# Six empty token columns taken out of a one-core streaming encoder: 1056 columns in chunks of 352 in place of 1062 in chunks of 354

## The chip, the cores and the metric

The kernel runs on one core of one Trainium2 chip. The metric is the device time of one execution in microseconds (us); the time of a kernel is the median over its runs, and one further execution was taken by the profiler. Engines are named as in the profile: PE is TensorE (PEld its weight loads), DVE VectorE, ACT ScalarE, POOL GpSimd, SP SyncE.

## The reference, cut to what matters

Two requests share one set of weights: a prompt of 1024 tokens and a sample of 32 tokens, each token a vector of 1024 features. Two layers:

- Layer 0: RMSNorm, an input projection into a state-space mixer and a windowed attention, an output projection, residual add.
- Layer 1: RMSNorm, then a short gated convolution: `z = C * V`, causal depthwise `conv3(z)` of width 3, times `B`, output projection, residual add.
- Both layers: RMSNorm, 4-head cross-attention into 256 memory tokens, residual add; RMSNorm, then a gated feed-forward of width 2816: `silu(conv3(h @ w_gate)) * (h @ w_val)`, down projection, residual add.
- A last RMSNorm.

The two convolutions run along tokens. The prompt's starts from two zero columns, the sample's from two stored columns, so that the two requests need two columns ahead of each.

## The kernel before, in words

Features lie on the 128 partitions, tokens along the free dimension: `X[P, 8, TW]` holds eight feature blocks of `TW` columns. `TW` is 1062: columns 0 to 1023 are the prompt, 1024 to 1029 (`SEQ:S0`) are empty, 1030 to 1061 the sample. Every product runs over all `TW` columns, cut into `NCH` = 3 chunks of `CW` = 354, one bank of PSUM each; six of the eight banks are two sets of three (`pset(0)`, `pset(1)`), which tiles use in turn.

Matrix products are in fp32 with both operands split in a high and a low part (`XH`, `XL` for activations, `WH`, `WL` for weights; `HH`, `HL` for the hidden values). So each step of a product is three matmuls, by `mms` (L981 to L983): high by high, low by high, high by low, each with a weight load of its own of 128x128.

- `tile_a` (used for up projections): 8 feature blocks x 3 chunks x 3 = 72 matmuls into one set.
- `down_tile` (down projections): 2 x 3 x 3 = 18 matmuls into one set.
- Weights stream from HBM in blocks: SP loads `WR`, ACT makes `WH` (L1672), POOL makes `WL` (L1575).

The phases follow in a fixed order: memory keys and values (`kv`), input projection and mixers (`inp`, `outb`, `glu`, `outa`), cross-attention `x0`, feed-forward `f0`, gated convolution `c1`, `x1`, `f1`. Each engine runs its own list, written out by hand; between engines there are semaphores. The class `Steps` gives the n-th increment of a semaphore a name, so `v.at("gate0", g)` is the point at which the step `gate0` of iteration `g` is done.

In a feed-forward group `g` (11 groups of two hidden blocks `e` = 0, 1) PE runs: gate tile of e = 0, the eight down tiles of the group before, value tile of e = 0, gate tile of e = 1, value tile of e = 1. DVE takes the gate tile out of PSUM into `G` (L864), makes the three taps of the convolution (`conv_taps`, L836 to L849: copy of the three tap weights to `FW`, copy of the two stored columns into `G`, one `tensor_scalar` and two `scalar_tensor_tensor` over `TW` columns into `TAP`), adds the down tiles to `X` (L891) in between, scales the SiLU that ACT made (L871), takes the value tile (L876) and makes the low part `HL` (L880). In the buffer `G` a block has `TW` + 2 columns: two zero columns, the prompt, and the stored columns of the sample in the last two of the six empty ones. PE waits for DVE where a set of banks must be free: the third down tile of a group, for one, waits for the add of the first (`(add[q], g * 8 + (j - 9))`).

The gated convolution `c1` has the same frame, with `C2` as the first product (L929), `G` as the second (L936), the taps, a scaling by `RSTD` in `TAP` (L939), and `HID` (L942).

Where the columns `SEQ:S0` would hold stale values, they are set to zero: `HH` and `HL` ahead of each cross-attention (L735, L736), `GY` in the first mixer (L716).

The names that the prediction follows: `CW`, `TW`, `S0` (L29 to L32), `mms`, `tile_a`, `down_tile` on PE, `gate`, `taps`, `scale`, `hid`, `tile` and `conv_taps` on DVE.

Of the kernel before, what the change touches and what calls it, by code (L numbers as in the profile page):

```python
# [21 lines left out]
ALU = mybir.AluOpType  # L22
# [3 lines left out]
P = 128  # L26
D, KT = 1024, 8
SEQ, DEC = 1024, 32
NCH, CW = 3, 354  # L29
TW = NCH * CW  # L30
# [63 lines left out]
def build(nc, a):  # L94
    with ExitStack() as ctx:
# [131 lines left out]
        G = put("G", [P, 2, TW + 2])  # L227
        TAP = put("TAP", [P, 2, TW])
        ACTV, HID = put("ACTV", [P, TW]), put("HID", [P, TW])
# [84 lines left out]
        glu_vec = Steps(sem("glu_vec"), [f"bl{j}" for j in four] + ["z"] + [f"gl{j}" for j in four]  # L314
                        + [s + str(j) for j in four for s in ("mul", "lo")])
        xv, xa, xp, xk, xc, xq, xe, xld, xz = {}, {}, {}, {}, {}, {}, {}, {}, {}
        ORDER = (("s", 2), ("a", 0), ("b", 1))
        for l in (0, 1):
# [35 lines left out]
        def _(dv):  # L354
# [475 lines left out]
            def conv_taps(s, e, wname, width, sname, i, filled, between=None):  # L830
# [13 lines left out]
                dv.scalar_tensor_tensor(out=TAP[:, e, :], in0=G[:, e, 1:TW + 1], scalar=FW[:, e, 1:2], in1=TAP[:, e, :],  # L844
# [4 lines left out]
                dv.scalar_tensor_tensor(out=TAP[:, e, :], in0=G[:, e, 0:TW], scalar=FW[:, e, 0:1], in1=TAP[:, e, :],  # L849
# [3 lines left out]
            def ffn(l, nxt):  # L853
# [4 lines left out]
                def gate(g, e, tile, first):  # L858
# [5 lines left out]
                    dv.tensor_tensor(tiled(G[:, e, 2:TW + 2]), pset(0), tiled(RSTD[:]), ALU.mult).then_inc(v.sem, 1)  # L864

# [49 lines left out]
            def conv(nxt):  # L915
# [7 lines left out]
                def tile(g, e, tc, tz, tb, pc, first, between=None):  # L923
                    dv.wait_ge(tile_done, tc)
                    if e == 1:
                        dv.wait_ge(*cv.at("zc0", g))
                    elif not first:
                        dv.wait_ge(*cv.at("zc1", g - 1))
# [7 lines left out]
                    dv.tensor_tensor(tiled(G[:, e, 2:TW + 2]), pset(pc[1]), tiled(C2[:]), ALU.mult).then_inc(cv.sem, 1)  # L936
                    conv_taps(cv, e, "cm_w", KT, "cm_s", g, f"zc{e}")
# [4 lines left out]
                    dv.tensor_tensor(tiled(HID[:]), pset(pc[2]), tiled(TAP[:, e, :]), ALU.mult).then_inc(cv.sem, 1)  # L942
# [726 lines left out]
        def _(act):  # L1669
# [214 lines left out]
            act.wait_ge(*glu_vec.at("z"))  # L1884
# [358 lines left out]
```

## Time and profile before

| what | value |
|---|---|
| median of 3 runs | 2974.7 us (2973.37 to 2975.24) |
| profiled execution, device time | 2973.88 us |
| its span, first to last instruction | 2972.1 us |
| instructions | 44233 |
| granted TensorE clock, mean | 0.991 of full speed |
| PE busy / PEld busy | 2899.5 us / 2833.2 us |
| DVE / ACT / POOL busy | 1551.7 / 773.6 / 756.4 us |

The page of the profile is of one execution on the chip. Busy time of PE counts from the start of a matmul to a modelled end, and matmuls overlap in it, so the cost of a matmul in a steady stretch is read from the distance of starts, not from its own length. A row of the timeline gives start, length, engine, line of the kernel, operation, tiles out<-in and the shapes out<-in. Idle time in square brackets is what lay ahead of the instruction on its engine, with what ended it.

### The profile page before, as it was taken

The numbers are of one execution on the slowest core, as the hardware profiler recorded it, in microseconds if no ns is written. First come the engines' busy times: TensorE is split into PE (matmuls) and PEld (weight loads), VectorE is DVE, ScalarE is ACT, GpSimd is POOL, SyncE is SP. The second block draws the span as 40 slices with busy tenths as digits, with TensorE's granted clock in tenths as the row PEclk, the third lists the DMA queues.
The fourth block names the chain that finished last, engine by engine and source line by source line (L and its number), as shares of the span: only waits on it lengthen the run. The fifth ranks groups of instructions, "written<-read, shape, count | busy, mean of one in ns | idle before, by whom it ended". The sixth has DMA issues, their size and how long they took to land.

```text
span 2972.1 us, 44233 instructions
## 1 busy us (share of the span) xinstructions
PE 2899.5 (98%) x18009; PEld 2833.2 (95%) x18009; DVE 1551.7 (52%) x1769; ACT 773.6 (26%) x1261; POOL 756.4 (25%) x350
## 2 busy tenths in 40 slices
PE   8999999999999999999999999999999999999996
PEld 8986799998999999999999999999899999999996
DVE  8867455556544445444463333555554544445444
ACT  6217644234311111111141111432341111111112
POOL 0106225122322112112152212521242112112113
PEclk9989999999999999999999999999999999999998
DMA  9273432110111111111111111121011111111111
GB/s 315 103 162 142 138 94 71 43 47 25 50 43 42 49 42 42 49 42 43 49 44 43 50 43 42 57 65 43 29 43 43 50 42 42 49 42 42 49 42 67
DMA packets 69132, 187.41 MB, mean 63 GB/s; under 512 B 7328, under 2 KB 25120, under 8 KB 67760
## 3 DMA queue, kind: packets, MB, share of 16 engines
q1 hardware_dynamic: 48928, 156.89, 15.4%
q10 hardware_dynamic: 20112, 29.22, 3.5%
q8 instruction: 66, 1.08, 0.1%
q14 instruction: 26, 0.21, 0.0%
HBM read 167.49 MB, written 21.61 MB: 64 GB/s over the span
## 4 chain that ended last, share of the span: by engine, by line
PE 93%; DVE 4%; ACT 2%; issue 1%; DMA 0%; DVEq 0%; POOL 0%; ACTq 0%; POOLq 0%; SPq 0%
PE PS L981 29%; PE PS L982 29%; PE PS L983 29%; PE PS L1125 2%; PE PS L1182 1%; PE PS L1145 0%; PE PS L1173 0%; PE PS L1022 0%; PE PS L1325 0%; DVE HL L761 0%; DVE XQL L755 0%; DVE XQL L749 0%; DVE X L811 0%; PE PS L1208 0%; ACT HH L1947 0%
## 5 line engine op out<-in xcount | busy, mean ns | idle before, releaser
L981 PE MATMUL PS<-XH,WH 128*128 128x354 f32 x3456 | 1127.6, 326 | 3.5 <-DVE X L710 1.1
L983 PE MATMUL PS<-XH,WL 128*128 128x354 f32 x3456 | 1121.8, 325 | 0.0
L982 PE MATMUL PS<-XL,WH 128*128 128x354 f32 x3456 | 1121.7, 325 | 0.0
L1575 POOL TENSOR_TENSOR WL<-WR,WH 128x1024 fp32r<-128x1024 f32 x216 | 529.4, 2451 | 2003.7 <-ACT WH L1672 2003.6
L981 PEld LDWEIGHTS PS<-XH,WH 128*128 128x128 f32 x3456 | 651.6, 189 | 7.7 <-DVE LNV L609 1.6
L982 PEld LDWEIGHTS PS<-XL,WH 128*128 128x128 f32 x3456 | 653.8, 189 | 1.2
L983 PEld LDWEIGHTS PS<-XH,WL 128*128 128x128 f32 x3456 | 649.9, 188 | 0.0
L1672 ACT ACTIVATE WH<-WR 128x1024 fp32r<-128x1024 f32 x216 | 228.9, 1060 | 1396.1 <-PE PS L983 1380.9
L981 PE MATMUL PS<-HH,WH 128*128 128x354 f32 x1662 | 543.9, 327 | 3.5 <-DVE X L811 2.1
L982 PE MATMUL PS<-HL,WH 128*128 128x354 f32 x1662 | 539.2, 324 | 0.0
L983 PE MATMUL PS<-HH,WL 128*128 128x354 f32 x1662 | 537.1, 323 | 0.0
L981 PEld LDWEIGHTS PS<-HH,WH 128*128 128x128 f32 x1662 | 312.5, 188 | 12.0 <-DVE X L891 4.7
L982 PEld LDWEIGHTS PS<-HL,WH 128*128 128x128 f32 x1662 | 314.3, 189 | 0.0
L983 PEld LDWEIGHTS PS<-HH,WL 128*128 128x128 f32 x1662 | 312.3, 188 | 0.0
L891 DVE TENSOR_TENSOR X<-X,PS 128x1062 f32<-128x1062 f32 x160 | 201.2, 1258 | 161.8 <-PE PS L983 161.8
L864 DVE TENSOR_TENSOR G<-PS,RSTD 128x1062 f32<-128x1062 f32 x44 | 55.6, 1264 | 391.2 <-PE PS L983 367.9
L876 DVE TENSOR_TENSOR HID<-PS,TAP 128x1062 f32<-128x1062 f32 x44 | 55.6, 1265 | 164.3 <-PE PS L983 164.1
L2013 ACT ACTIVATE ACTV<-TAP 128x1062 f32<-128x1062 f32 x44 | 48.2, 1095 | 336.0 <-DVE TAP L849 336.0
L880 DVE TENSOR_TENSOR HL<-HID,HH 128x1062 fp32r<-128x1062 f32 x44 | 119.7, 2722 | 25.5 <-ACT HH L2018 25.5
L1584 POOL TENSOR_TENSOR RSTD<-RSTD,SQ 128x1062 f32<-128x1062 f32 x42 | 117.8, 2804 | 18.8 <-ACT SQ L1689 16.4
L871 DVE TENSOR_TENSOR TAP<-ACTV,RSTD 128x1062 f32<-128x1062 f32 x44 | 95.5, 2169 | 29.4 <-ACT ACTV L2013 29.4
L811 DVE TENSOR_TENSOR X<-X,PS 128x1062 f32<-128x1062 f32 x48 | 59.9, 1258 | 67.1 <-PE PS L983 67.1
(326 smaller groups left out, 2767.1 us busy)
## 6 DMA issues: line engine op xcount, KB each, us to landing
WR<-in_w SPq DMA_DIRECT2D x224, 512.0 KB, 3.2
WK<-in_w SPq DMA_DIRECT2D x16, 512.0 KB, 4.8
XR<-in_x ACTq DMA_DIRECT2D x8, 531.0 KB, 7.0
X<-in_x SPq DMA_DIRECT2D x8, 531.0 KB, 7.1
out_y<-X SPq DMA_DIRECT2D x8, 531.0 KB, 3.1
WX<-in_w SPq DMA_DIRECT2D x8, 512.0 KB, 5.3
CM<-scratch_cm SPq DMA_DIRECT2D x2, 2048.0 KB, 9.9
scratch_uj<-UJ ACTq DMA_DIRECT2D x1, 2128.0 KB, 7.0
```

Source lines behind the costliest of these rows:

```text
L811: dv.tensor_tensor(tiled(X[:, m, :]), tiled(X[:, m, :]), pset(m % 2), ALU.add).then_inc(add[q], 1)
L864: dv.tensor_tensor(tiled(G[:, e, 2:TW + 2]), pset(0), tiled(RSTD[:]), ALU.mult).then_inc(v.sem, 1)
L871: dv.tensor_tensor(TAP[:, e, :], ACTV[:], RSTD[:], ALU.mult).then_inc(v.sem, 1)
L880: dv.tensor_tensor(HL[:, e, :], HID[:], HH[:, e, :].bitcast(F32), ALU.subtract).then_inc(v.sem, 1)
L891: dv.tensor_tensor(tiled(X[:, m, :]), tiled(X[:, m, :]), pset((1 + m) % 2), ALU.add).then_inc(add[q], 1)
L981: pe.matmul(out, h, rh, start=start, stop=False)
L982: pe.matmul(out, h, rl, start=False, stop=False)
L983: return pe.matmul(out, l, rh, start=False, stop=stop)
L1125: mm = pe.matmul(o, l, r, start=k == 0, stop=k == KT - 1, skip_group_check=True)
L1575: pool.tensor_tensor(WL[:, s, :], WR[:, s, :], WH[:, s, :].bitcast(F32), ALU.subtract).then_inc(w_lo, 1)
L1584: pool.tensor_tensor(RSTD[:], RSTD[:], sq, ALU.add).then_inc(n_sum[q], 1)
L1672: act.activation(WH[:, s, :], WR[:, s, :], ACT.Copy).then_inc(w_hi, 1)
```

## The change

The six empty columns are dropped: `CW` is 352, `TW` 1056, and the sample begins at column 1024, right behind the prompt. Only the convolutions' buffers keep two columns between prompt and sample: `G` has `TW` + 4 columns a block, `TAP` and `ACTV` have `TW` + 2. The taps run over 1058 columns. Where a step joins a buffer with the gap and one without it, it is now two instructions, one over the prompt's side and one over the sample's 32 columns: taking `G` out of PSUM, the scaling after the SiLU, and in `c1` the scaling by `RSTD`, which is written to `C2` and no more in place. The first instruction that fills `G` still writes all `TW` columns, and the second then writes the sample's over again, two columns further on. The zeroings of `SEQ:S0` go away. The core of the diff:

```diff
-NCH, CW = 3, 354
+NCH, CW = 3, 352
...
-        G = put("G", [P, 2, TW + 2])
-        TAP = put("TAP", [P, 2, TW])
-        ACTV, HID = put("ACTV", [P, TW]), put("HID", [P, TW])
+        G = put("G", [P, 2, TW + 4])
+        TAP = put("TAP", [P, 2, TW + 2])
+        ACTV, HID = put("ACTV", [P, TW + 2]), put("HID", [P, TW])
...
-                if c == 7:
-                    dv.memset(GY[:, :, SEQ:S0], 0.0).then_inc(glu_vec.sem, 1)
...
-                dv.memset(HH[:, :, SEQ:S0].bitcast(F32), 0.0).then_inc(xz[l], 1)
-                dv.memset(HL[:, :, SEQ:S0].bitcast(F32), 0.0).then_inc(xz[l], 1)
-                dv.wait_ge(xz[l], 2)
...
-                dv.tensor_copy(G[:, e, S0:S0 + 2], sc[:, bass.ds(f, 1), :].rearrange("p o k -> p (o k)")).then_inc(s.sem, 1)
+                dv.tensor_copy(G[:, e, SEQ + 2:SEQ + 4], sc[:, bass.ds(f, 1), :].rearrange("p o k -> p (o k)")).then_inc(s.sem, 1)
                 dv.wait_ge(*s.at(f"st{e}", i))
-                dv.tensor_scalar(TAP[:, e, :], G[:, e, 2:TW + 2], FW[:, e, 2:3], None, ALU.mult).then_inc(s.sem, 1)
+                dv.tensor_scalar(TAP[:, e, :], G[:, e, 2:TW + 4], FW[:, e, 2:3], None, ALU.mult).then_inc(s.sem, 1)
...
                     dv.tensor_tensor(tiled(G[:, e, 2:TW + 2]), pset(0), tiled(RSTD[:]), ALU.mult).then_inc(v.sem, 1)
+                    dv.wait_ge(*v.at(f"prompt{e}", g))
+                    dv.tensor_tensor(G[:, e, S0 + 4:TW + 4], PS[:, 2, CW - DEC:CW], RSTD[:, S0:TW], ALU.mult).then_inc(v.sem, 1)
...
-                    dv.tensor_tensor(TAP[:, e, :], ACTV[:], RSTD[:], ALU.mult).then_inc(v.sem, 1)
+                    dv.tensor_tensor(TAP[:, e, 0:SEQ], ACTV[:, 0:SEQ], RSTD[:, 0:SEQ], ALU.mult).then_inc(v.sem, 1)
+                    dv.tensor_tensor(TAP[:, e, S0:TW], ACTV[:, S0 + 2:TW + 2], RSTD[:, S0:TW], ALU.mult).then_inc(v.sem, 1)
...
                     if e == 1:
-                        dv.wait_ge(*cv.at("zc0", g))
+                        dv.wait_ge(*cv.at("hid0", g))
                     elif not first:
-                        dv.wait_ge(*cv.at("zc1", g - 1))
+                        dv.wait_ge(*cv.at("hid1", g - 1))
...
-                    dv.tensor_tensor(TAP[:, e, :], TAP[:, e, :], RSTD[:], ALU.mult).then_inc(cv.sem, 1)
+                    dv.tensor_tensor(C2[:, 0:SEQ], TAP[:, e, 0:SEQ], RSTD[:, 0:SEQ], ALU.mult).then_inc(cv.sem, 1)
+                    dv.tensor_tensor(C2[:, S0:TW], TAP[:, e, S0 + 2:TW + 2], RSTD[:, S0:TW], ALU.mult).then_inc(cv.sem, 1)
...
-            act.wait_ge(*glu_vec.at("z"))
+            act.wait_ge(*glu_vec.at("bl3"))
```

The step that used to be called `gate` is now `prompt`, and `gate` is the sample's instruction behind it, so that whoever waited for `gate0` waits for both; in `c1` the same holds for `zp` and `zc`, and `cp` and `cr`.

## Rows read from the trace of the kernel before

**Rows 1.** The page's busy times: us, share of the span, instructions.

```profile
PE 2899.5 (98%) x18009; PEld 2833.2 (95%) x18009; DVE 1551.7 (52%) x1769; ACT 773.6 (26%) x1261; POOL 756.4 (25%) x350
```

**Rows 2.** The page's chain that ended last, share of the span by engine.

```profile
PE 93%; DVE 4%; ACT 2%; issue 1%; DMA 0%; DVEq 0%; POOL 0%; ACTq 0%; POOLq 0%; SPq 0%
```

**Rows 3.** Stretches: us; busy us (count) of PE, PEld, DVE, ACT, POOL; clock; DMA.

```profile
495.00:740.00 245.00, 234.87 (x1522) 226.75 (x1521) 131.53 (x267) 85.78 (x178) 61.67 (x27) 1.00 0.14 46
740.00:1507.00 767.00, 766.38 (x4701) 762.81 (x4700) 377.27 (x290) 137.71 (x172) 176.10 (x71) 1.00 0.13 45
```

**Rows 4.** Groups by line on PE, shapes apart: count | busy us, mean ns.

```profile
L981 PE MATMUL PS<-XH,WH 128*128 128x354 f32 x3456 | 1127.6, 326 | 3.5 <-DVE X L710 1.1 <-DVE LNV L609 1.0 <-ACT KVS L1725 0.8
L981 PE MATMUL PS<-HH,WH 128*128 128x354 f32 x1662 | 543.9, 327 | 3.5 <-DVE X L811 2.1 <-DVE HL L761 0.9 <-ACT UG L1869 0.5
L981 PE MATMUL PS<-GH,WH 128*128 128x354 f32 x48 | 15.6, 325 | 0.0
L1447 PE MATMUL PS<-HH,WH 128*128 128x354 f32 x18 | 5.8, 325 | 0.0
```

**Rows 5.** Timeline on PE, f0: first matmuls of two tiles, 72 starts apart.

```profile
1465.30 0.32 PE L981 MATMUL PS<-XH,WH 128*128 128x354 f32 x1
...
1476.99 0.33 PE L981 MATMUL PS<-XH,WH 128*128 128x354 f32 x1
```

**Rows 6.** Timeline on PE, kv: matmuls of 256 columns, 35 starts apart.

```profile
29.79 0.28 PE L981 MATMUL PS<-MH,WH 128*128 128x256 f32 x1
...
33.97 0.28 PE L983 MATMUL PS<-MH,WLX 128*128 128x256 f32 x1
```

**Rows 7.** Timeline on PE, x0: matmuls of 512 columns, 9 starts apart.

```profile
538.67 0.40 PE L983 MATMUL PS<-HH,VXL 128*128 128x512 f32 x1
...
540.75 0.39 PE L983 MATMUL PS<-HH,VXL 128*128 128x512 f32 x1
```

**Rows 8.** Timeline on PE, x0: matmuls of 32 columns, 11 starts apart.

```profile
525.27 0.26 PE L981 MATMUL PS<-HH,VXH 128*128 128x32 f32 x1
...
526.50 0.26 PE L983 MATMUL PS<-HH,VXL 128*128 128x32 f32 x1
```

**Rows 9.** Timeline, f0, all engines: a gate tile's end to the third down tile.

```profile
1442.03 1.26 DVE L864 TENSOR_TENSOR G<-PS,RSTD 128x1062 f32<-128x1062 f32 x1 [7.14 <-PE PS L983]
...
1443.16 2.40 POOL L1575 TENSOR_TENSOR WL<-WR,WH 128x1024 fp32r<-128x1024 f32 x1 [9.40 <-ACT WH L1672]
...
1443.21 2.38 DVE L836 COPY FW<-COL 128x3 f32 x1
...
1445.69 0.77 DVE L840 TENSOR_SCALAR TAP<-G,FW 128x1062 f32<-128x1062 f32 x1
...
1446.38 1.25 DVE L891 TENSOR_TENSOR X<-X,PS 128x1062 f32<-128x1062 f32 x1
...
1447.42 0.33 PE L983 MATMUL PS<-HH,WL 128*128 128x354 f32 x1
1447.68 0.43 PE L981 MATMUL PS<-HH,WH 128*128 128x354 f32 x1
1447.95 0.32 PE L982 MATMUL PS<-HL,WH 128*128 128x354 f32 x1
```

**Rows 10.** Groups on DVE by line, shapes apart: the nearest small operations.

```profile
L787 DVE TENSOR_TENSOR HL<-PS,HH 128x64 fp32r<-128x64 f32 x8 | 1.7, 217 | 0.0
...
L404 DVE TENSOR_TENSOR ERP<-PR 128x32 f32<-128x32 f32 x1 | 0.2, 197 | 0.0
```

**Rows 11.** Timeline on DVE: the last scaling and last value tile of f0.

```profile
1498.54 1.26 DVE L871 TENSOR_TENSOR TAP<-ACTV,RSTD 128x1062 f32<-128x1062 f32 x1 [1.24 <-ACT ACTV L2013]
1500.66 1.26 DVE L876 TENSOR_TENSOR HID<-PS,TAP 128x1062 f32<-128x1062 f32 x1 [0.86 <-PE PS L983]
```

**Rows 12.** Timeline on PE, x0: 256 columns of HH, 11 starts apart.

```profile
547.49 0.28 PE L981 MATMUL PS<-HH,VXH 128*128 128x256 f32 x1
...
548.79 0.28 PE L983 MATMUL PS<-HH,VXL 128*128 128x256 f32 x1
```

More of the change, by code:

```diff
@@ L313, in build @@
                         + [s + str(j) for j in four for s in ("sig", "hi")])
-        glu_vec = Steps(sem("glu_vec"), [f"bl{j}" for j in four] + ["z"] + [f"gl{j}" for j in four]
+        glu_vec = Steps(sem("glu_vec"), [f"bl{j}" for j in four] + [f"gl{j}" for j in four]
                         + [s + str(j) for j in four for s in ("mul", "lo")])
-        xv, xa, xp, xk, xc, xq, xe, xld, xz = {}, {}, {}, {}, {}, {}, {}, {}, {}
+        xv, xa, xp, xk, xc, xq, xe, xld = {}, {}, {}, {}, {}, {}, {}, {}
         ORDER = (("s", 2), ("a", 0), ("b", 1))
@@ L334, in build @@
             xe[l] = Steps(sem(f"x{l}_queries"), [f"e{j}" for j in range(2 * NCH)])
-            xld[l], xz[l] = sem(f"x{l}_kv_loads"), sem(f"x{l}_zeroed")
+            xld[l] = sem(f"x{l}_kv_loads")
         fv, fa, fz = {}, {}, {}
         for l in (0, 1):
-            fv[l] = Steps(sem(f"f{l}_vec"), ["gate0", "w0", "st0", "a0", "b0", "c0", "sm0", "hid0", "gate1", "lo0", "w1", "st1",
-                                             "a1", "b1", "c1", "sm1", "hid1", "lo1"])
+            fv[l] = Steps(sem(f"f{l}_vec"), ["prompt0", "gate0", "w0", "st0", "a0", "b0", "c0", "sp0", "sm0", "hid0", "prompt1", "gate1", "lo0",
+                                             "w1", "st1", "a1", "b1", "c1", "sp1", "sm1", "hid1", "lo1"])
             fa[l] = Steps(sem(f"f{l}_act"), [s + str(e) for e in (0, 1) for s in ("silu", "na", "nb", "hi")])
             fz[l] = sem(f"f{l}_zeroed")
-        cv = Steps(sem("c1_vec"), [s + str(e) for e in (0, 1) for s in ("cc", "zc", "w", "st", "a", "b", "c", "cr", "hid", "lo")])
+        cv = Steps(sem("c1_vec"), [s + str(e) for e in (0, 1) for s in ("cc", "zp", "zc", "w", "st", "a", "b", "c", "cp", "cr", "hid", "lo")])
         ca = Steps(sem("c1_act"), [s + str(e) for e in (0, 1) for s in ("na", "nb", "hi")])
@@ L843, in conv_taps @@
                 dv.wait_ge(*s.at(f"a{e}", i))
-                dv.scalar_tensor_tensor(out=TAP[:, e, :], in0=G[:, e, 1:TW + 1], scalar=FW[:, e, 1:2], in1=TAP[:, e, :],
+                dv.scalar_tensor_tensor(out=TAP[:, e, :], in0=G[:, e, 1:TW + 3], scalar=FW[:, e, 1:2], in1=TAP[:, e, :],
                                         op0=ALU.mult, op1=ALU.add).then_inc(s.sem, 1)
@@ L848, in conv_taps @@
                 dv.wait_ge(*s.at(f"b{e}", i))
-                dv.scalar_tensor_tensor(out=TAP[:, e, :], in0=G[:, e, 0:TW], scalar=FW[:, e, 0:1], in1=TAP[:, e, :],
+                dv.scalar_tensor_tensor(out=TAP[:, e, :], in0=G[:, e, 0:TW + 2], scalar=FW[:, e, 0:1], in1=TAP[:, e, :],
                                         op0=ALU.mult, op1=ALU.add).then_inc(s.sem, 1)
@@ L875, in hid @@
                     dv.wait_ge(*v.at(f"sm{e}", g))
-                    dv.tensor_tensor(tiled(HID[:]), pset(1), tiled(TAP[:, e, :]), ALU.mult).then_inc(v.sem, 1)
+                    dv.tensor_tensor(tiled(HID[:]), pset(1), tiled(TAP[:, e, 0:TW]), ALU.mult).then_inc(v.sem, 1)
                 def low(g, e):
@@ L2000, in new_states @@
                 act.activation(STF[:, 0:2, bass.ds(g * 2 + e, 1)].rearrange("p s o -> p (s o)"), G[:, e, SEQ:SEQ + 2], ACT.Copy).then_inc(s.sem, 1)
-                act.activation(STF[:, 2:4, bass.ds(g * 2 + e, 1)].rearrange("p s o -> p (s o)"), G[:, e, TW:TW + 2], ACT.Copy).then_inc(s.sem, 1)
+                act.activation(STF[:, 2:4, bass.ds(g * 2 + e, 1)].rearrange("p s o -> p (s o)"), G[:, e, TW + 2:TW + 4], ACT.Copy).then_inc(s.sem, 1)
             def ffn(l, nxt):
```

4 lines of the change are left out of this document (3 added, 1 removed).

## The prediction

> **What bounds the kernel now.** The busy times come first [rows 1]: PE is busy for 98% of the span and its weight loads for 95%, while DVE stands at 52% and ACT and POOL at a quarter. The reader is to see that one engine fills the span and that the others have room. Busy time of PE overlaps itself, so the chain that ended last is the check: 93% of it is PE, 4% DVE, 2% ACT [rows 2]. The windows then show where: in the first feed-forward, 767 us long, PE is busy for 766.38 us at a granted clock of 1.00, which is 2.4 GHz; in the first cross-attention it idles for 10 of 245 us [rows 3]. So in the feed-forwards and the gated convolution the time is the number of matmuls times their spacing, and the few per cent of chain on DVE and ACT lie where phases meet and inside the cross-attentions.
>
> **What a matmul costs, and what two columns of it cost.** The grouped view gives the counts [rows 4]: 3456 + 1662 + 48 + 18 = 5184 rows of first products, each with two siblings of equal count, so 15552 matmuls of 354 columns that the change makes 352 wide. Their spacing: 72 starts in 1476.99 - 1465.30 = 11.69 us, 162.4 ns [rows 5]. The same kind of product at other widths: 256 columns in (33.97 - 29.79) / 35 = 119.4 ns [rows 6], 512 columns in (540.75 - 538.67) / 9 = 231.1 ns [rows 7]. The slope from 256 to 354 is 43.0 / 98 = 0.439 ns a column, from 354 to 512 it is 68.7 / 158 = 0.435. The three widths lie on one line; two columns are worth 0.87 ns. With the other 256-column stretch, (548.79 - 547.49) / 11 = 118.2 ns [rows 12], the lower slope is 0.451 and the two columns 0.90. I take 0.87.
>
> The line could fail below, if the weight load set the spacing: every one of these matmuls brings a 128x128 load. The 32-column matmuls bring the same load and start every (526.50 - 525.27) / 11 = 111.8 ns [rows 8], so the load allows 112 ns where 354 columns take 162, and the columns are what is paid. The Trainium skill speaks against this: its page Perfetto Trace Analysis, section Identifying the Most-Contended Engine, says that the headroom of TensorE is judged by the busy share of its weight loads rather than of its matmuls; by that rule 95% would leave little for narrower matmuls to give.
>
> The whole saving is 15552 x 0.87 = 13.5 us. The Trainium skill's page TensorE: Matmul & The Clock Gate, section Back-to-back issue gap, gives N/2.4 + 2.5 ns for an isolated warm matmul, an estimate of 13.0 us here; the rows above have a steeper slope and are used.
>
> **What of it is not on the path.** In a feed-forward group the third down tile waits for the add of the first. PE's starts 1447.42, 1447.68, 1447.95 are 0.26 and 0.27 us apart in place of 0.16, so 0.2 us of waiting a group [rows 9]. The add starts at 1446.38 and takes 1.25, to 1447.63, and what leads up to it isn't PE: POOL's `WL` from 1443.16 to 1445.56, the copy to `FW` that ends at 1445.59, the first tap from 1445.69 (0.77), the add. None of these has fewer columns by more than 0.6%. The two tiles of 18 matmuls ahead of the wait then arrive 36 x 0.87 = 31 ns earlier and wait 31 ns longer: over the 20 groups of both feed-forward loops 0.6 us is lost. Likewise some 6% of the chain runs over DVE and ACT [rows 2]; matmuls beside it give nothing to the end. An estimate: 6% of 13.5, 0.8 us, is lost there; against it stand the full-width operations of that part, by my guess half of 6% of 2972, 89 us, which shrink by 6/1062, 0.5 us. Net 0.3 us.
>
> **What is added.** Each of the 44 gate tiles and 8 convolution tiles gets two more DVE instructions over 32 columns. The trace has 217 ns for 64 columns with one operand in PSUM and 197 ns for 32 in SBUF [rows 10]; with the wait on its own engine I take 0.25 us each, 104 x 0.25 = 26 us of DVE, which is idle for half of the span. Where it is put matters more. Behind the gate's second part DVE has the copy to `FW`, the taps and the adds, and PE's third tile waits for them. At present the `FW` copy of three columns is issued at 1443.21 and takes 2.38 us, to the moment when POOL's `WL` is through [rows 9]: it is held by POOL. Issued 0.25 us later it ends at the same time, and the gate's second part costs nothing. If that cover were gone it would cost 20 x 0.25 = 5 us. The second part of the scaling stands ahead of a wait for PE's value tile: in the last group, which has least room, the scaling ends at 1499.80 and the value tile is taken at 1500.66 after 0.86 us of idling [rows 11]. 0.25 us fits twice. Those two gaps are all that hides the new work. The gate tile's banks come free 0.25 us later, at about 1443.5, and the second down tile, which writes them, starts only some 2.9 us after the gate tile's end. In `c1` the product into `C2` now waits for `hid`, which stands ahead of it on the same engine anyhow.
>
> The removed zeroings are of a few columns, on DVE, while PE has tiles of 11.7 us to run; removing them and the changed wait of ACT gives nothing. The loads of `x` and stores of `y` shrink by 0.6% and lie beside other work or in the last microseconds; I count nothing.
>
> **The sum.** -13.5 + 0.6 + 0.3 = -12.6 us on the profiled execution's 2973.9 us (span 2972.1 and 1.8 around it): 2961.3 us. The median of the runs is 0.8 us above that execution, so the forecast could read 2962.1 by it; that is within its uncertainty. By itself this case would lie between 2958 and 2965.
>
> **Rivals.**
>
> *The moving operand is read in groups, and 354 pays for a part-filled one.* 354 is no multiple of four, 352 is one of 32. With groups of four columns, 354 pays for 356 and the change takes off four columns' worth, 1.75 ns: 27 us less, and with the same losses about 2948. For it: of the three widths measured, 354 alone isn't a multiple of four. Against it: the line through 256 and 512 gives 119.4 + 98 x 0.436 = 162.1 at 354, the row says 162.4, and 356 columns' worth would be 163.0. Between, so it stays in play.
>
> *The new DVE instructions come onto the path.* If the `FW` copy isn't covered by POOL, or the first tap loses its rate (0.77 us for 1062 columns, where the others take about 1.25), 5 to 10 us of the gain go into the third down tile's wait: 2966 to 2971. Against it: a cover of 2.1 us for 0.25, and an even number of columns as before.
>
> *The weight loads set the pace after all*, and narrower matmuls change nothing: 2974. For it the 95% [rows 1]; against it the 32-column rows [rows 8].
>
> *Slower: the rows' places in SBUF.* A row of `XH` is 4248 bytes now and a chunk 1416, so that chunk starts are spread modulo 64 bytes; after the change, 4224 and 1408, all lie alike. If alike is bad for the reads, each matmul pays. The memory-side rows at a stride of 1024 bytes take 119.4 ns [rows 6], the `HH` rows at 4248 take 118.2 [rows 12]: 1.2 ns, which at 352 columns would be 1.65, 25.7 us in all, and net 13 us slower: 2986. The point that decides is 0.87 ns a matmul. Against it: the first of these stretches is the start of the kernel, where other engines also hand over between blocks.
>
> **Chances and range.** The forecast 0.67, the grouped read 0.14, the DVE wait 0.08, no change by weight loads 0.04, slower by place 0.07. The range 2948 to 2967 reaches to the grouped read and leaves out half of it, the worse half of the DVE case, and the last two: about 2 in 10. A difference of 0.2%, 6 us, is about what a measurement can tell from no change. Faster by more: 0.67 + 0.14 + half of 0.08 = 0.85. Within: the other half and the weight loads, 0.08. Slower: 0.07.
>
> **What would show it.** The 72 starts of an up tile take 11.63 us, 161.5 ns a matmul; 11.56 would be the grouped read, 11.69 the weight loads, more the places. The third down tile's two starts are together 0.23 us late in place of 0.20; 0.45 would be the lost cover. The `FW` copy of e = 0 ends with POOL's `WL` and shows about 2.1 us; the first tap stays at 0.77. DVE has some 100 more instructions and about as much busy time, and PE keeps its 93% of the chain. The prediction is wrong if the spacing doesn't follow the line, or if PE shows waits for `G` or `TAP` that are not there now.

## The result and the profile after

The changed kernel takes 2943.8 us (median of 4 runs, 2940.75 to 2946.0), the kernel before 2974.7 on the same chip: a ratio of 0.9893 (95% interval 0.9881 to 0.9905). It is 31 us faster where 13 were forecast, and the time lies below the range. The profiled execution took 2943.9 us, with a span of 2942.1.

The page's busy times and its chain by engine, of the kernel after:

```profile
PE 2859.0 (97%) x18009; PEld 2787.4 (95%) x18009; DVE 1562.9 (53%) x1868; ACT 771.9 (26%) x1261; POOL 765.7 (26%) x350
...
PE 84%; DVE 6%; POOL 4%; issue 3%; ACT 2%; DMA 1%; DVEq 0%; POOLq 0%; ACTq 0%; SPq 0%
```

PE keeps its 18009 matmuls and loses 40.5 us of busy time against [rows 1]; DVE has 99 instructions more. The chain tells that something else happened too: PE's share fell from 93% to 84%, and POOL, which had none [rows 2], has 4%.

Windows over the same matmuls as [rows 3], of the kernel after: us, then busy us (count) of PE, PEld, DVE, ACT, POOL, granted clock, DMA.

```profile
492.20:737.90 245.70, 234.04 (x1522) 225.61 (x1521) 131.70 (x267) 85.28 (x178) 63.53 (x28) 0.99 0.14 46
737.90:1493.40 755.50, 753.02 (x4701) 747.99 (x4700) 381.18 (x334) 137.70 (x172) 176.92 (x71) 1.00 0.14 46
```

The first feed-forward is 11.5 us shorter at the same granted clock of 1.00, that is 2.4 GHz, and PE, which idled for 0.6 us of it, now idles for 2.5. The cross-attention, with 1522 matmuls as before, gained nothing: 245.7 us for 245.0.

Timeline on PE, kernel after: first matmuls of two tiles 72 starts apart, in `f0` and in `c1`.

```profile
1452.50 0.32 PE L982 MATMUL PS<-XH,WH 128*128 128x352 f32 x1
...
1463.94 0.32 PE L982 MATMUL PS<-XH,WH 128*128 128x352 f32 x1
...
1711.13 0.32 PE L982 MATMUL PS<-XH,WH 128*128 128x352 f32 x1
...
1722.65 0.32 PE L982 MATMUL PS<-XH,WH 128*128 128x352 f32 x1
```

11.44 us over 72 is 158.9 ns in `f0`, 11.52 is 160.0 ns in `c1`; [rows 5] gave 162.4, and the forecast was 161.5. Here is the surplus. Spacings below are worked out in this way, or as means of all starts less than 185 ns apart in a block.

Timeline on DVE and on PE, kernel after: a gate tile's end to the third down tile, as in [rows 9].

```profile
1429.57 1.26 DVE L859 TENSOR_TENSOR G<-PS,RSTD 128x1056 f32<-128x1056 f32 x1 [6.89 <-PE PS L984]
1430.86 0.19 DVE L861 TENSOR_TENSOR G<-PS,RSTD 128x32 f32<-128x32 f32 x1
1431.00 2.13 DVE L831 COPY FW<-COL 128x3 f32 x1
...
1433.24 0.77 DVE L835 TENSOR_SCALAR TAP<-G,FW 128x1058 f32<-128x1058 f32 x1
1433.93 1.25 DVE L889 TENSOR_TENSOR X<-X,PS 128x1056 f32<-128x1056 f32 x1
...
1434.82 0.32 PE L984 MATMUL PS<-HH,WL 128*128 128x352 f32 x1
1435.23 0.43 PE L982 MATMUL PS<-HH,WH 128*128 128x352 f32 x1
1435.50 0.32 PE L983 MATMUL PS<-HL,WH 128*128 128x352 f32 x1
```

The new instruction (L861, 0.19 us) is covered as forecast: the copy to `FW` starts later, takes 2.13 us in place of 2.38 and ends at the same distance behind the gate. The tile's two starts are 0.41 and 0.27 us apart, 0.36 us of waiting for 0.20 before: DVE's chain has kept its length, and PE comes to it earlier.

Timelines on POOL: adds of the last norm, where nothing runs beside them. Three of the kernel before, then three of the kernel after.

```profile
2930.11 2.06 POOL L1584 TENSOR_TENSOR RSTD<-RSTD,SQ 128x1062 f32<-128x1062 f32 x1 [0.41 <-ACT SQ L1689]
2933.21 2.49 POOL L1584 TENSOR_TENSOR RSTD<-RSTD,SQ 128x1062 f32<-128x1062 f32 x1 [1.04 <-ACT SQ L1689]
2936.13 2.07 POOL L1584 TENSOR_TENSOR RSTD<-RSTD,SQ 128x1062 f32<-128x1062 f32 x1 [0.43 <-ACT SQ L1689]
```

```profile
2900.50 2.47 POOL L1585 TENSOR_TENSOR RSTD<-RSTD,SQ 128x1056 f32<-128x1056 f32 x1 [0.40 <-ACT SQ L1690]
2903.53 2.47 POOL L1585 TENSOR_TENSOR RSTD<-RSTD,SQ 128x1056 f32<-128x1056 f32 x1 [0.56 <-ACT SQ L1690]
2906.39 2.49 POOL L1585 TENSOR_TENSOR RSTD<-RSTD,SQ 128x1056 f32<-128x1056 f32 x1 [0.39 <-ACT SQ L1690]
```

`SQ` has two rows, used in turn. Before, they lay 4248 bytes apart, and the add took 2.07 us on one row and 2.49 on the other. Now they lie 4224 bytes apart, a multiple of 64, and every add takes the longer time, with six columns less to do. At a norm between two blocks PE waits for the end of this chain. Timelines on POOL and on PE, kernel after, from `f0` to `c1`:

```profile
1509.93 13.81 POOL L1585 TENSOR_TENSOR RSTD<-RSTD,SQ 128x1056 f32<-128x1056 f32 x4
1523.71 4.70 POOL L1576 TENSOR_TENSOR WL<-WR,WH 128x1024 fp32r<-128x1024 f32 x2
...
1523.89 1.37 PE L1023 MATMUL PS<-RSTD,ONES 128*128 128x352 f32 x4
1526.11 0.43 PE L982 MATMUL PS<-XH,WH 128*128 128x352 f32 x1 [0.86 <-POOL WL L1576]
```

`WL` of the next tile stands behind the adds in POOL's queue, and PE's next product needs it. From the last start of the sum over partitions (L1023) to the first product it is 1.32 us here. At the five norms between blocks that distance was 0.03, 0.03, 0.37, 0.36 and 0.03 us before, and is 1.31 to 1.33 after: 5.8 us.

PE's order of matmuls is the same in all kernels, so the starts of two traces can be laid side by side. Differences to the profiled execution before, us, with some runs of the next section. The first column sums what starts less than 185 ns apart gained, the second the five norms, the third the waits at the down tiles of both feed-forwards:

| kernel | spacing | norms | down tiles | other | total |
|---|---|---|---|---|---|
| after | -43.9 | +5.8 | +3.6 | +4.6 | -29.9 |
| before, 352 wide | -9.9 | +0.1 | +0.6 | +2.1 | -7.1 |
| after, rows 8 bytes further apart | -9.5 | +5.2 | +1.7 | +4.2 | +1.6 |
| after, add first | -49.9 | +5.7 | -3.0 | +8.1 | -39.1 |
| after, `RSTD` moved | -39.2 | -0.7 | +2.0 | +2.1 | -35.8 |
| after, both | -36.6 | -0.7 | -4.2 | +1.3 | -40.2 |

### The profile page after: what moved, and what is told of

Same layout as the page of the kernel before. It is cut to its first block, busy times and chain, and to the rows that moved or that the text cites. A ratio compares the mean times of both kernels' runs of the same rounds, so it can differ in the third digit from the quotient of the medians.

```text
span 2942.1 us, 44372 instructions
## 1 busy us (share of the span) xinstructions
PE 2859.0 (97%) x18009; PEld 2787.4 (95%) x18009; DVE 1562.9 (53%) x1868; ACT 771.9 (26%) x1261; POOL 765.7 (26%) x350
## 4 chain that ended last, share of the span: by engine, by line
PE 84%; DVE 6%; POOL 4%; issue 3%; ACT 2%; DMA 1%; DVEq 0%; POOLq 0%; ACTq 0%; SPq 0%
PE PS L982 26%; PE PS L984 26%; PE PS L983 26%; POOL RSTD L1585 3%; PE PS L1126 2%; DVE G L859 1%; DVE X L889 1%; PE PS L1183 1%; PE PS L1146 0%; PE PS L1174 0%; PE PS L1326 0%; POOL WL L1576 0%; DVE HL L756 0%; DVE XQL L744 0%; DVE XQL L750 0%
## 5 line engine op out<-in xcount | busy, mean ns | idle before, releaser
L982 PE MATMUL PS<-XH,WH 128*128 128x352 f32 x3456 | 1119.8, 324 | 9.9 <-POOL WL L1576 4.3
L984 PE MATMUL PS<-XH,WL 128*128 128x352 f32 x3456 | 1112.0, 322 | 0.0
L983 PE MATMUL PS<-XL,WH 128*128 128x352 f32 x3456 | 1109.6, 321 | 0.0
L982 PE MATMUL PS<-HH,WH 128*128 128x352 f32 x1662 | 540.3, 325 | 6.6 <-DVE X L806 3.3
L984 PE MATMUL PS<-HH,WL 128*128 128x352 f32 x1662 | 534.4, 322 | 0.0
L983 PE MATMUL PS<-HL,WH 128*128 128x352 f32 x1662 | 533.4, 321 | 0.0
L889 DVE TENSOR_TENSOR X<-X,PS 128x1056 f32<-128x1056 f32 x160 | 200.5, 1253 | 156.8 <-PE PS L984 156.8
L1585 POOL TENSOR_TENSOR RSTD<-RSTD,SQ 128x1056 f32<-128x1056 f32 x42 | 129.6, 3087 | 14.6 <-ACT SQ L1690 11.4
L878 DVE TENSOR_TENSOR HL<-HID,HH 128x1056 fp32r<-128x1056 f32 x44 | 119.6, 2717 | 25.4 <-ACT HH L2019 25.4
L868 DVE TENSOR_TENSOR TAP<-ACTV,RSTD 128x1024 f32<-128x1024 f32 x44 | 94.1, 2139 | 29.3 <-ACT ACTV L2014 29.3
L806 DVE TENSOR_TENSOR X<-X,PS 128x1056 f32<-128x1056 f32 x48 | 59.6, 1251 | 65.7 <-PE PS L984 65.7
```

What stands on the lines that cost most here:

```text
L806: dv.tensor_tensor(tiled(X[:, m, :]), tiled(X[:, m, :]), pset(m % 2), ALU.add).then_inc(add[q], 1)
L868: dv.tensor_tensor(TAP[:, e, 0:SEQ], ACTV[:, 0:SEQ], RSTD[:, 0:SEQ], ALU.mult).then_inc(v.sem, 1)
L878: dv.tensor_tensor(HL[:, e, :], HID[:], HH[:, e, :].bitcast(F32), ALU.subtract).then_inc(v.sem, 1)
L889: dv.tensor_tensor(tiled(X[:, m, :]), tiled(X[:, m, :]), pset((1 + m) % 2), ALU.add).then_inc(add[q], 1)
L982: pe.matmul(out, h, rh, start=start, stop=False)
L983: pe.matmul(out, h, rl, start=False, stop=False)
```

## The experiments

**Width alone, places alone, unequal widths.** Three kernels ask where the spacing came from: the kernel before with products of 352 columns at the old starts; the changed kernel with its moving operands' rows 1058 columns apart, 8 bytes more; the changed kernel with two of three chunks wider.

```diff
 # before, 352 wide (f0, c1, f1; the last two columns of each chunk are left out)
-mm = mms(PS[:, 3 * pset_i + c, 0:CW], wh, wl, chunk(H[:, k, :], c), chunk(L[:, k, :], c),
+mm = mms(PS[:, 3 * pset_i + c, 0:352], wh, wl, H[:, k, c * CW:c * CW + 352], L[:, k, c * CW:c * CW + 352],
 # after, rows 8 bytes further apart (the same for XL, HH, HL)
-XH = place("XH", [P, KT, TW], F32R)
+XH = place("XH", [P, KT, TW + 2], F32R)[:, :, 0:TW]
```

> The kernel before, rows of 1062 columns and chunk starts as they were, but the products of f0, c1 and f1 (11808 matmuls) read and write only the first 352 columns of each chunk; the last two columns of a chunk keep what the banks held, so the output is left wrong there. Two theories for why a matmul fell from 162.4 to about 159.3 ns in the changed kernel. Places: 0.87 ns of it are the two columns, the other 2.2 ns come from where rows and chunks begin in SBUF; then the tile of 72 starts takes 161.5 ns a matmul here, and the time is about 2964 us. Width: a width of 354 is itself costly and 352 is not (groups of columns, or a width that isn't a multiple of 32); then 159.3 ns here too, and about 2946 us.

Measured: 2967.0 us, ratio 0.9967 (0.9956 to 0.9978), spacing 161.5 ns in all three blocks. Timeline on PE of this kernel, 72 starts, 161.4 ns apart:

```profile
1465.51 0.32 PE L991 MATMUL PS<-XH,WH 128*128 128x352 f32 x1
...
1477.13 0.32 PE L991 MATMUL PS<-XH,WH 128*128 128x352 f32 x1
```

At the old starts two columns are worth 0.9 ns, as the line of the prediction said. The grouped read falls as the prediction had it, with four columns paid for from any start. Groups that lie fixed in memory aren't excluded by this run: over starts that are spread, their cost would average out to a price by the column.

> The changed kernel with rows of XH, XL, HH, HL 1058 columns apart (two columns of padding, so that rows begin 8 bytes further on modulo 64 each time); every matmul is 352 wide as before and the result is the same. Places: the tile of 72 starts goes back to about 161.5 ns a matmul, and the time to about 2966 us. Width: 159.3 ns and 2944 us, as without padding.

Measured: 2975.9 us, ratio 1.0003 (0.9993 to 1.0012), spacing 161.7 to 161.8 ns. The same columns, widths and instructions, and by 8 bytes a row the whole gain in time is gone. Timeline on PE of this kernel, 72 starts, 161.4 ns apart:

```profile
1465.33 0.32 PE L982 MATMUL PS<-XH,WH 128*128 128x352 f32 x1
...
1476.95 0.32 PE L982 MATMUL PS<-XH,WH 128*128 128x352 f32 x1
```

> The changed kernel, but the first two of the three chunks are read wider than they need be, 354 columns in f0, 360 in f1, 368 in c1 (the extra columns go to unused places of the bank; the result is the same). Starts stay where they are. Places, with 0.437 ns a column: f0 159.9, f1 161.6, c1 164.0 ns a matmul, and about 2968 us. Width in groups of four: f0 160.5; in groups of eight: f0 161.6, the same as f1.

Measured: 2989.1 us, ratio 1.0051 (1.0034 to 1.0068), spacing 163.0 ns in `f0`, 165.2 in `c1`, 163.7 in `f1`. That is more than the columns account for. It led to theory R, a rhythm of like matmuls, which the next four were meant to test.

**Equal narrower, equal wider, all 8 bytes on, rows 32 bytes further apart.**

```diff
 # narrower: 350 in f0, 344 in c1, 336 in f1; wider: 354, 360, 368, third chunk from 688
+def chunk_w(x, c, wide):
+    return x[:, c * CW:c * CW + wide]
 # all 8 bytes on (the same for XL, HH, HL)
-XH = place("XH", [P, KT, TW], F32R)
+XH = place("XH", [P, KT * TW + 2], F32R)[:, 2:].rearrange("p (k t) -> p k t", k=KT)
```

> The changed kernel, with the products of the first feed-forward block 350 columns wide, those of the middle block 344 and those of the last block 336, all three chunks alike and at the old starts (0, 352, 704); the columns beyond are left uncomputed. Theory R (matmuls that are all equally wide and whose reads all start alike modulo 64 bytes fall into a strict period, and nothing more is asked of the width): one start to the next 158.0 ns (350), 155.4 ns (344), 151.9 ns (336), each at most 1 to 2 ns above when a wait has disturbed it, and the whole about 2898 us. Rival M (the width itself has to be a multiple of 16 or 32 columns): 350 and 344 lose the gain of some 2.2 ns and stand at 160.6 and 158.0 ns, 336 at 151.9 ns, the whole about 2913 us. If only the multiple of 32 counts, 336 stands at 154.5 ns too.

Measured: 2915.3 us, 0.9797 (0.9781 to 0.9813); 160.0 ns at 350, 156.7 at 344, 153.3 at 336. This doesn't decide: 344 lies midway between R (155.4) and M (158.0), 350 lies nearer to M, and so does the time. From 344 to 336 a column is worth 3.33 / 8 = 0.417 ns in this execution.

> The changed kernel, with its four moving operands (XH, XL, HH, HL) starting 8 bytes later in their places, rows still 1056 columns apart: every read starts alike, 8 bytes behind a multiple of 64. The result is the same. Theory R (alike among themselves is enough): spacing 158.9 to 160.0 ns in the feed-forward blocks and 2944 us. Rival A (each read has to start on a multiple of 16, 32 or 64 bytes itself): spacing 161.5 to 162 ns, as with rows 8 bytes further apart, and 2965 to 2976 us.

Measured: 2987.0 us, 1.0037 (1.0024 to 1.0049); 162.3 ns at the up tiles, 162.9 at the down tiles. The gain is gone, but this isn't the test of R that it was meant to be: the kernel's `place` rounds each buffer's size up to 32 bytes, so that `XL` and `HL`, each behind a buffer that grew by 8 bytes, start 40 bytes behind a multiple of 64, and only `XH` and `HH` start at 8. The reads weren't all alike. R falls further on, where all reads of a tile start alike at 8, 24 or 32 bytes.

> The changed kernel with the products 354 columns wide in the first feed-forward block, 360 in the middle one and 368 in the last, all three chunks alike, and the third chunk starting at column 688 instead of 704, so that all starts stay on multiples of 64 bytes; the surplus products are read by nobody, and the third chunk's columns come out displaced. Theory R: the gain stays at the old width: spacing 159.8 ns (354), 162.4 ns (360), 165.9 ns (368), the whole about 2983 us. Rival M (a width that is no multiple of 16 or 32 columns loses the gain): 162.4 ns at 354 (the kernel before's figure), 165.0 ns at 360, and at 368 (a multiple of 16, not of 32) 165.9 or 168.5 ns, the whole 3000 to 3013 us.

Measured: 2997.4 us, 1.0078 (1.0061 to 1.0095); up tiles 162.2 ns at 354, 164.4 at 360, 167.0 at 368. Timeline on PE, `f0`, 72 starts, 162.2 ns apart:

```profile
1458.78 0.33 PE L993 MATMUL PS<-XH,WH 128*128 128x354 f32 x1
...
1470.46 0.33 PE L993 MATMUL PS<-XH,WH 128*128 128x354 f32 x1
```

Neither forecast fits as a whole: 354 and 360 lie nearer to M's figures, and 368 lies 1.1 ns above R's. For the account of the change this is the run of the old width at starts on multiples of 64 bytes: 162.2 ns, where 354 columns at the old starts took 162.4. The starts alone bring nothing, as little as the width alone; the 163.0 ns of the run with two chunks of 354 are then mostly the price of 354 columns.

> The changed kernel with the rows of its four moving operands 1064 columns apart instead of 1056, so that the rows of odd tiles start 32 bytes behind a multiple of 64. The result is the same. If what counts is the start modulo 64 bytes (or that all are alike modulo 64): spacing 161.5 to 162 ns and 2970 to 2976 us, as with rows 8 bytes further apart. If the start modulo 32 bytes or less counts: 158.9 to 160.0 ns and 2944 us.

Measured: 2961.2 us, 0.9951 (0.9935 to 0.9968); 160.8 to 160.9 ns. A start of 32 bytes in every second row takes a good part of the gain, not all. Neither figure was expected.

**The start in steps, and pieces of a read.**

> The kernel with all moving operands 8 bytes behind a multiple of 64 (352 columns took 162.3 ns there), with products 350 columns wide in the first feed-forward block, 344 in the middle one, 342 in the last; the columns beyond are left uncomputed. Theory B (what a product costs is the number of 32-byte pieces, 8 columns, that its read touches: 44 pieces 158.9 to 160.0 ns, 45 pieces 162.3 ns, 43 pieces 155.6 to 156.7 ns): 350 columns touch 44 pieces and fall by over 2 ns to 158.9 to 160.0, 344 touch 44 too and stay there, 342 touch 43 and stand at 155.6 to 156.7 ns; some 2943 us. With pieces of 16 bytes: 158.9 to 160.0, 157.2 to 158.3, 156.7. Rival L (a start off the multiple of 64 costs a fixed 2.3 ns, and the width counts by the column, 0.42 ns): 161.5, 159.0 and 158.2 ns; some 2955 us.

Measured: up tiles 161.1, 159.3 and 158.3 ns, 2955.8 us, in one execution. `XL` and `HL` lie 40 bytes behind a multiple of 64 here too, which changes nothing in B's count of 32-byte pieces. L is within 0.4 ns each; B is off by 1.1 and more at 350 and 342. Against 160.0 and 156.7 ns from starts at 0, the start costs 1.1 ns at 350 columns and 2.6 at 344, so it isn't L's fixed price either.

> The changed kernel with XH and XL (the operands of the up tiles) 32 bytes behind a multiple of 64 and HH and HL (those of the down tiles) 16 bytes behind one, all rows 1056 columns apart; the result is the same. Theory B with 32-byte pieces: up tiles 158.9 to 160.0 ns (44 pieces), down tiles 162.3 ns (45 pieces). With 16-byte pieces both 158.9 to 160.0 ns. If a start has to lie on a multiple of 64: both 161.5 to 162.5 ns. Times about 2950, 2944 and 2980 us.

Measured: up tiles 161.1 ns, down tiles 160.0, 2961.7 us, in one execution. The places aren't those named: by the rounding of `place`, `XL` starts at 0 (`XH` at 32) and `HL` at 48 (`HH` at 16). 160.0 is a figure of starts at 0, and so, in runs further on, is 161.1; the run shows that 16 and 48 bytes needn't cost anything, and leaves 32 open. Two kernels then left the buffers in their places, all at multiples of 64, and gave each block and each kind of tile a start of its own, all 344 wide.

```diff
+WIDE = {"f0": ((344, 2), (344, 4)), "c1": ((344, 0), (344, 8)), "f1": ((344, 4), (344, 2))}   # up, down: width, start
+def chunk_w(x, c, wide):
+    return x[:, c * CW + wide[1]:c * CW + wide[1] + wide[0]]
```

> The changed kernel with all products of the three large blocks 344 columns wide (the other columns are left uncomputed and the columns read are displaced), so that each block's up tiles and down tiles can have a start of their own behind a multiple of 64 bytes: first block up 8 bytes, down 16; middle block up 0, down 32; last block up 16, down 8. From a start at 0, 344 columns took 156.7 ns. Theory 16 (a start on a multiple of 16 bytes costs nothing, any other some 2 ns): 155.6 to 157.8 ns at 0, 16 and 32 bytes, 158.5 to 159.5 ns at 8. Theory 64 (only a multiple of 64 is free): 158 to 159.5 ns at 8, 16 and 32 alike. If neither: 16 bytes stays with 0, and 32 stands between.

> As the run with starts 8/16, 0/32, 16/8, with the places exchanged: first block up 32 bytes, down 0; middle block up 8, down 16; last block up 24, down 32 (344 columns everywhere in them, the rest left uncomputed). Theory 16: 155.6 to 157.8 ns at 0, 16 and 32 bytes, 158.5 to 159.5 ns at 8 and at 24. Theory 64: 158 to 159.5 ns at all but 0. A start that has one figure in one place and another in the other would show that the start is not what sets it.

Timeline on PE of the first of the two: 36 starts of down tiles or 72 of up tiles between two rows, pair by pair.

```profile
1365.44 0.32 PE L993 MATMUL PS<-HH,WH 128*128 128x344 f32 x1
...
1371.06 0.32 PE L993 MATMUL PS<-HH,WH 128*128 128x344 f32 x1
...
1447.71 0.32 PE L993 MATMUL PS<-XH,WH 128*128 128x344 f32 x1
...
1459.16 0.32 PE L993 MATMUL PS<-XH,WH 128*128 128x344 f32 x1
...
1689.33 0.32 PE L993 MATMUL PS<-HH,WH 128*128 128x344 f32 x1
...
1695.05 0.32 PE L993 MATMUL PS<-HH,WH 128*128 128x344 f32 x1
...
1703.15 0.32 PE L993 MATMUL PS<-XH,WH 128*128 128x344 f32 x1
...
1714.44 0.32 PE L993 MATMUL PS<-XH,WH 128*128 128x344 f32 x1
```

That is 156.1 ns from a start at 16 bytes, 159.0 at 8, 158.9 at 32, 156.8 at 0. Over both kernels (2923.8 and 2935.1 us): 156.7 and 156.8 at 0; 156.2, 156.3 and 156.4 at 16; 158.9, 159.0 and 158.9 at 8; 158.9 at 24; 158.9, 158.9 and 158.8 at 32. Each start has its figure wherever it stands, up or down. Each kernel ran once, and blocks of one execution can differ about as much with all starts alike (the last runs below); but up and down tiles alternate within a block, and in all five blocks where one kind starts at 0 or 16 bytes and the other at 8 or 32, the second takes at least 2 ns longer. So the start sets it; by what rule stays open, since 16 is free and 32 is not. R falls: every read of an up tile starts alike at 8, and the 2 ns are lost. M falls: 344 is no multiple of 16, and has the gain. B falls: from 16 bytes 344 columns touch 44 pieces of 32 bytes and cost least, from 32 bytes they touch 43 and cost 2 ns more.

> The changed kernel with every start on a multiple of 64 bytes and six widths: first block up 350, down 348; middle block up 352, down 344; last block up 346, down 340 (the columns beyond are left uncomputed). By the column (0.42 ns each, from 160.0 or 158.9 ns at 352): 159.2 or 158.1 at 350, 158.3 or 157.2 at 348, 157.5 or 156.4 at 346, 156.7 or 155.6 at 344, 155.0 or 153.9 at 340. In steps of 4 columns: 160.0 at 350, 158.3 at 348 and 346, 156.7 at 344, 155.0 at 340 (each or 1.1 less). In steps of 8 columns: 160.0 at 350, 348 and 346, 156.7 at 344 and 340.

Measured, from starts at 0: 158.9 ns at 352, 160.0 at 350, 158.8 at 348, 160.0 at 346, 157.0 at 344, 155.6 at 340; 2940.9 us. 346 columns took longer than 352, but they stand in different blocks, and runs below show one kernel's 352 columns at 158.9 ns in one block and 161.1 in another. By the column, and in steps of 4, 346 doesn't fit, even with 1.1 ns either way; steps of 8 do, for all six, with that allowance. The down tiles at 348 had two figures themselves (158.2 and 160.0). That the width counts in steps isn't shown.

**What the change gives back.** Two repairs, of the third down tile's wait and of POOL's adds.

```diff
 # the first down add ahead of the copy and the taps
-                    taps(g, 0, None if first else down_add)
+                    if not first:
+                        down_add(0)
+                    taps(g, 0, None if first else lambda j: down_add(j + 1))
 # RSTD 24 bytes later
-        RSTD = place("RSTD", [P, TW])
+        RSTD = place("RSTD", [P, TW + 6])[:, 6:]
```

> The changed kernel, but in the feed-forward groups the add of the first down tile stands ahead of the three taps' first instructions (the FW copy that POOL's lock holds), and the second and third adds one place earlier. If the third down tile's wait in the changed kernel (two starts 0.39 and 0.27 us apart in place of 0.16) is the chain by way of POOL, it goes away and 20 groups x 0.34 = 6.8 us are won: about 2937 us. Rival: the wait moves to the next tile, whose add now stands behind the held copy, and the time stays at 2944 us.

Measured: 2939.4 us, 0.9887 (0.9870 to 0.9903). The wait at the third down tile is gone, and the matmuls of `f0` take 4.9 us less than after the change, 3.5 of it waits and 1.5 closer starts (158.9 ns throughout). Timeline on PE at the third down tile, whose starts were 0.41 and 0.27 us apart:

```profile
1432.76 0.32 PE L986 MATMUL PS<-HH,WL 128*128 128x352 f32 x1
1432.92 0.32 PE L984 MATMUL PS<-HH,WH 128*128 128x352 f32 x1
1433.08 0.32 PE L985 MATMUL PS<-HL,WH 128*128 128x352 f32 x1
```

Timeline on DVE: the add now runs before the copy that POOL used to hold, and the copy takes 0.16 us behind it.

```profile
1428.80 0.19 DVE L861 TENSOR_TENSOR G<-PS,RSTD 128x32 f32<-128x32 f32 x1
1430.37 1.25 DVE L889 TENSOR_TENSOR X<-X,PS 128x1056 f32<-128x1056 f32 x1 [1.37 <-PE PS L986]
...
1431.54 0.16 DVE L831 COPY FW<-COL 128x3 f32 x1
```

> The changed kernel with one place moved: RSTD, the accumulator of the sum of squares, starts 24 bytes later. Nothing else, and the result is the same. Theory P (what the change gives back at the five norm transitions is GpSimd's chain of adds RSTD = RSTD + SQ: two operands whose rows start alike cost 2.47 us, 24 bytes apart 2.07 us; before, one of SQ's two rows was 24 bytes off): the seven adds of a transition fall from 22.3 to between 18.5 and 20.2 us, TensorE's wait between the sum over partitions and the first product from 1.32 to under 0.4 us, five times, so 5 to 6.5 us less: 2937 to 2939 us. Rival W (the wait comes of TensorE being faster, not of a slower chain): adds and gaps as in the changed kernel, 2944 us.

Measured: 2938.3 us, 0.9878 (0.9862 to 0.9895). Theory P holds: the adds and the waits are shorter. Timelines on POOL and on PE of this kernel, from `f0` to `c1` and in the last norm:

```profile
1507.62 12.18 POOL L1585 TENSOR_TENSOR RSTD<-RSTD,SQ 128x1056 f32<-128x1056 f32 x4
1519.76 2.38 POOL L1576 TENSOR_TENSOR WL<-WR,WH 128x1024 fp32r<-128x1024 f32 x1
...
1521.63 1.35 PE L1023 MATMUL PS<-RSTD,ONES 128*128 128x352 f32 x4
1522.55 0.59 PE L982 MATMUL PS<-XH,WH 128*128 128x352 f32 x1
...
2894.80 2.06 POOL L1585 TENSOR_TENSOR RSTD<-RSTD,SQ 128x1056 f32<-128x1056 f32 x1 [0.40 <-ACT SQ L1690]
2897.83 2.06 POOL L1585 TENSOR_TENSOR RSTD<-RSTD,SQ 128x1056 f32<-128x1056 f32 x1 [0.97 <-ACT SQ L1690]
```

The add takes 2.06 us on both rows of `SQ`, and `WL` ends before PE needs it: the five distances are 0.03 us each. The longer `RSTD` also moved all that lies behind it by 32 bytes, `SQ` with it, so that the two operands lie 8 bytes apart modulo 64 here, not 24. A run further on with 64 bytes of room, where `SQ` keeps its place and they lie 24 apart, has the same 2.06 us and 0.03 us.

> The two repairs together: the first down add ahead of the copy and the taps (2939.4 us by itself, the wait ahead of the third down tile gone) and RSTD 24 bytes later. If both costs were separate waits on TensorE's path: 5 to 6.5 us below the first repair alone, 2933 to 2935 us, all starts of the feed-forward blocks 158.9 ns apart. If the transitions' wait has another cause: 2939 us.

Measured: 2934.6 us, 0.9864 (0.9848 to 0.9881), the lowest median of this study. The medians fall by 4.4 and 5.5 us with one repair and by 9.2 with both, but the intervals of the single repairs overlap with that of the change by itself, and the first repair's four times lie up to 12 us apart. What the traces show is firmer: by the table above, norms and down tiles together wait 6.7 us less with the first repair, 8.1 with the second and 14.3 with both. With both, the spacing was 160.0 ns throughout where the first repair alone had shown 158.9, which takes part of this back, so three runs asked to whom these steps belong; the third has `TW + 16` in place of `TW + 6`.

> The first repair (the down add ahead of the copy and the taps) once more, profiled anew. Its first profiled execution ran at 158.9 ns in all three large blocks, and its four times lay between 2934.9 and 2946.8 us. If the step of the period (158.9, 160.0 or 161.1 ns) is drawn anew in each execution, this one may show another step, and its time goes with it, 17 us from one step to the next over 15,552 products. If the step belongs to the kernel: 158.9 ns and 2935 us again.

> Both repairs once more, the same kernel as before, profiled anew. If the step of the period is drawn anew in each execution, it may show another than 160.0 ns, and its time goes with it. If the step belongs to the kernel: 160.0 ns in all three large blocks and 2932 to 2936 us.

> Both repairs, with RSTD 24 bytes later as before, but with 64 bytes of room behind it, so that all that lies further on in SBUF keeps its place modulo 64 bytes (in the run with both repairs it moved by 32). If those places set the step of the period: 158.9 ns as in the first repair alone and some 2922 us. If not: 160.0 ns or a mixture, 2933 to 2935 us.

Timeline on PE of the first: 72 starts in `f0`, then 72 in `f1`.

```profile
1445.13 0.32 PE L984 MATMUL PS<-XH,WH 128*128 128x352 f32 x1
...
1456.58 0.32 PE L984 MATMUL PS<-XH,WH 128*128 128x352 f32 x1
...
2435.84 0.32 PE L984 MATMUL PS<-XH,WH 128*128 128x352 f32 x1
...
2447.44 0.32 PE L984 MATMUL PS<-XH,WH 128*128 128x352 f32 x1
```

158.9 ns in `f0`, 161.1 in `f1`, where the same kernel had shown 158.9 in both: 2941.5 us for 2934.9. So the kernel doesn't fix the step. Within one execution it can change too: after the change, 29 of the undisturbed up tiles of `f0` ran at 158.9 ns and 12 at 160.0. Both repairs repeated gave 160.0 ns in all blocks again (2934.9 us); with 64 bytes of room 160.0, 161.1 and 160.0 (2935.6 us, 0.9861, 0.9844 to 0.9877). This gives no sign that places further on decide it; what does stays open.

## Why the prediction was wrong

**The bound was right.** PE's matmuls set the time, and narrower ones shortened it. The weight loads aren't the bound: spacing fell by over 3 ns with loads of the same size. The Trainium skill's page Perfetto Trace Analysis, section Identifying the Most-Contended Engine, judges TensorE's headroom by MFU (the share of its peak rate) and by the busy share of its weight loads; by the second, 95% would be little headroom. The trace disagrees, with PEld at 95% again and PE's starts closer.

**The step that failed is the price of two columns.** "The three widths lie on one line; two columns are worth 0.87 ns" took each spacing for a function of the width. At the old starts it was: 0.9 ns in the run of 352 columns there. But the change also moved every chunk start onto a multiple of 64 bytes, and from such starts 354 columns took 162.2 ns and 352 took 158.9 to 161.1, mostly 158.9 or 160.0. Neither the width alone (161.5 ns) nor the starts alone (162.2) come near to what both did to the 162.4 ns of before. The saving per matmul was 43.9 / 15388 = 2.85 ns in place of 0.87. The price of a start depends on the width: some 0.2 ns at 354 columns, 1.1 at 350, and at 344 2.0 to 2.8 ns between starts at 0 or 16 bytes and those at 8, 24 or 32. Why two columns are worth so much from these starts stays open. The rival of the places in SBUF named half of the cause, with the wrong sign. Its support, [rows 6] against [rows 12], set two different stretches side by side and no start against another. Of the starts the Trainium skill's page SBUF — State Buffer, section Operand start alignment, asks only that they be multiples of the element size, calls this a matter of legality, and timed nothing; rows 8 bytes further apart obey it and lose the whole gain in time here.

**The term "not on the path" was too small by an order of magnitude.** For the down tiles 0.6 us were forecast by the right mechanism (PE arrives earlier at a DVE chain of fixed length); it became 3.6 us. Of that, 36 x 3.2 ns x 20 groups = 2.3 us follow from the larger saving by the forecast's own working; the rest isn't sorted. For the joints of the phases 0.3 us net were forecast, by the guess that full-width operations shrink by 6/1062. POOL's adds grew instead, by 0.4 us on one of `SQ`'s rows: 5.8 us at five norms. This is shown, since moving `RSTD` by 24 bytes takes it away, with what lies behind it moved by 32 or left in place. The remaining 4.6 us lie spread over the phases; no run here sorts them, and the phases ahead of the first cross-attention alone differ by 3.9 us between the two executions of the first repair.

**Two errors of opposite sign.** With the old spacing law and the new waits the change would have brought nothing: the run with rows 8 bytes further apart has 9.5 us of saving, waits that eat it, and a ratio of 1.0003. That the kernel became faster, as forecast, is owed to the starts, which the prediction had as a possible loss: the direction was luck.

**What held.** The new DVE instructions are hidden; the first tap stays at 0.77 us, the copy to `FW` still ends with POOL's `WL`, DVE's busy time rose by 11 us. The grouped read of four columns from any start fell. The DVE wait didn't come from the new instructions; it grew because PE came earlier.

## What to carry to other kernels

A change of a width in a packed layout is also a change of every row's and chunk's place: list the start of each operand modulo 64 bytes before and after, and price the places apart from the width, with one kernel that has the new width at the old starts and one that has the old width at the new starts. Work out the starts from the allocator, with its rounding, also in the kernels of the experiments. Where the engine that sets the time gets faster, look at each queue that hands it work: an operation off the path whose operands moved too (here GpSimd's adds) can become the wait. An add that frees PSUM for TensorE goes ahead of work that another engine can hold up.

## What had not been expected of the hardware

- A 344-column fp32r matmul in a steady stream starts every 156.1 to 156.8 ns when its moving operand begins 0 or 16 bytes behind a multiple of 64, and every 158.8 to 159.0 ns at 8, 24 or 32 bytes.
- With starts on multiples of 64 bytes, 354 columns took 162.2 ns a matmul and 352 took 158.9 to 161.1; with starts spread over multiples of 8 bytes, 162.4 and 161.5.
- A stream of 352-column matmuls ran at 158.9, 160.0 or 161.1 ns, constant over whole tiles, and the same kernel showed different steps in two executions and in tiles of one.
- GpSimd's add of two 1056-column fp32 rows took 2.47 us with both operands at multiples of 64 bytes, and 2.06 us with one at 24 bytes behind a multiple and the other at 0 or 32.
